# HGRN recurrence of a hybrid decoder step: eight slots a head joined to five

## The reference

```
b = jnp.cumsum(gc, axis=1)
o_inter = jnp.einsum('bthk,bhkv->bthv', qc * jnp.exp(b), S)
decay = jnp.where(tri, jnp.exp(jnp.where(tri, diff, 0.0)), 0.0)      # diff = b_t - b_s
att = jnp.einsum('bthk,bshk,btshk->bhts', qc, kc, decay)
o_intra = jnp.einsum('bhts,bshv->bthv', att, vc)
S = jnp.exp(b_last)[..., None] * S + jnp.einsum('bshk,bshv->bhkv', kc * jnp.exp(b_last[:, None] - b), vc)
```

## Time and profile before

| | us |
|---|---|
| median of 3 runs | 1181.65 |
| lowest and highest | 1181.28, 1184.76 |
| span of the profiled execution | 1185.2 |
| PE busy | 1123.6 (95%) |
| DVE busy | 703.2 (59%) |
| ACT busy | 536.1 (45%) |
| POOL busy | 172.4 (15%) |

### The profile page before, as it was taken

One profiled execution on the slowest core, in us unless ns is written; L12 is line 12 of the kernel. 1 busy time (PEld: TensorE's weight loads), 2 busy tenths in 40 slices (PEclk: granted clock), 3 DMA queues, 4 the chain that ended last, 5 costly groups with the idle time before them and its releaser, 6 DMA issues.

```text
span 1185.2 us, 21987 instructions
## 1 busy us (share of the span) xinstructions
PE 1123.6 (95%) x8805; PEld 1059.3 (89%) x8805; DVE 703.2 (59%) x1440; ACT 536.1 (45%) x951; POOL 172.4 (15%) x137
## 2 busy tenths in 40 slices
PE   5898999998999989999999999899999999999997
PEld 4797889876899978989989999699999999999997
DVE  5735555445487767477788554736464555537465
ACT  3433556465546664755555423543323232232324
POOL 1400000000132213213121001321101010010101
PEclk9899999988999989999999999899999999999998
DMA  9884333212322311221322373032322322322202
GB/s 309 268 291 139 109 106 107 74 37 71 116 90 75 109 54 61 69 84 63 110 64 73 100 251 113 2 108 72 105 74 72 107 72 72 97 81 72 73 35 81
DMA packets 108922, 120.53 MB, mean 102 GB/s; under 512 B 2708, under 2 KB 98796, under 8 KB 108533
## 3 DMA queue, kind: packets, MB, share of 16 engines
q1 hardware_dynamic: 108821, 119.13, 31.1%
HBM read 109.29 MB, written 11.80 MB: 102 GB/s over the span
## 4 chain that ended last, share of the span: by engine, by line
PE 45%; DVE 3%; ACT 1%; issue 1%; POOL 0%; DVEq 0%; ACTq 0%; POOLq 0%
PE PS L860 41%; PE PS L833 1%; DVE wR L1448 1%; PE PS L983 0%; PE PS L773 0%; PE PS L782 0%; DVE tmp L1432 0%; PE PS L1055 0%; PE PS L806 0%; POOL hR L1767 0%; ACT wR L1116 0%; DVE xhat L1416 0%; DVE xT L1465 0%; PE PS L1022 0%; ACT hR L1185 0%
## 5 line engine op out<-in xcount | busy, mean ns | idle before, releaser
L860 PE MATMUL PS<-hR,wR 128*128 128x288 f32 x3744 | 528.4, 299 | 1.9 <-DVE mods L1476 1.0
L860 PEld LDWEIGHTS PS<-hR,wR 128*128 128x128 f32 x3744 | 505.6, 189 | 11.6 <-issue 9.6
L1448 DVE TENSOR_TENSOR wR<-raw,wR 128x512 fp32r<-128x512 f32 x260 | 213.6, 821 | 84.5 <-ACT wR L1116 77.2
L860 PE MATMUL PS<-actR,wR 128*128 128x288 f32 (+2 forms) x1920 | 260.9, 297 | 1.8 <-DVE actR L1596 1.8
L860 PEld LDWEIGHTS PS<-actR,wR 128*128 128x128 f32 x1920 | 257.0, 189 | 3.0 <-DVE actR L1596 2.0
L1116 ACT ACTIVATE wR<-raw 128x512 fp32r<-128x512 f32 x260 | 164.3, 632 | 141.6 <-PE PS L860 132.9
L1782 POOL TENSOR_TENSOR D<-b 128x512 f32<-128x512 f32 (+1 forms) x48 | 59.5, 1239 | 484.6 <-PE PS L948 264.2
L1809 POOL TENSOR_TENSOR actR<-tmp,actR 128x576 fp32r<-128x576 f32 x32 | 46.3, 1448 | 304.7 <-DVE actR L1511 304.7
L1511 DVE CAST actR<-tmp 128x576 fp32r<-128x576 f32 x32 | 15.2, 476 | 125.7 <-ACT tmp L1227 125.7
L815 PE MATMUL PS<-wR,hR 128*128 128x256 f32 x600 | 78.9, 288 | 0.0
L815 PEld LDWEIGHTS PS<-wR,hR 128*128 128x128 f32 x600 | 74.4, 193 | 2.1 <-issue 1.7
(11 more groups left out here) (227 smaller groups left out, 1189.4 us busy)
## 6 DMA issues: line engine op xcount, KB each, us to landing
raw<-in_w_in SPq DMA_DIRECT2D x30, 1024.0 KB, 5.1
raw<-in_w_up SPq DMA_DIRECT2D x16, 1024.0 KB, 5.5
raw<-in_w_down SPq DMA_DIRECT2D x16, 1024.0 KB, 4.9
mid<-in_w_ada SPq DMA_DIRECT2D x12, 1024.0 KB, 5.0
ada<-in_w_ada SPq DMA_DIRECT2D x8, 1024.0 KB, 11.9
S<-in_state_hgrn SPq DMA_DIRECT2D x8, 512.0 KB, 4.4
out_hgrn_sample<-S SPq DMA_DIRECT2D x8, 512.0 KB, 4.9
raw<-in_w_out SPq DMA_DIRECT2D x4, 1024.0 KB, 5.1
```

Source lines behind the costliest of these rows:

```text
L860: mm = pe.matmul(PS[:, 2 * x.pair + h, 0:size], weights(x, w, k, col), rhs[r], start=(k == 0 and n == 0), stop=(k == last and n == 2))
L1448: done(dve.tensor_tensor(w[:, 1, cols], raw[SLOT[SPLITS[n]]][:, cols], w[:, 0, cols].bitcast(F32), ALU.subtract), s_lo)
```

## The change

Only `hgrn_slots` changes. Before, each head has eight slots: one for each level, with the other events hung on them, one of the two sample halves with level 5 and the other with the output, then the norm. Now a head has five: the diagonal with levels 0 and 1 and `g_hats`; levels 2 and 3 with the keys; level 4, the state and level 5; both sample halves with the output; the norm. One of the two empty slots at the start of a pair is gone too, so that a pair has 13 slots in place of 20, spread over the same chunks. Within a level the order of the events is kept, and so is the distance, counted in levels, at which operands, exponents and differences run ahead.

```
-        for k in range(NL + 2):
-            ev = []
-            if k == 0:
-                ev += [("g_diag", r)]
-            if k < NL:
-                n = (r - first) * NL + k
...
-            if k == 1:
-                ev += [("g_hats", r)]
-            if k == 3:
-                ev += [("g_keys", r)]
-            if k == 4:
-                ev += [("g_state", r)]
-            if k in (5, 6):
-                ev += [("g_sample", r, k - 5)]
...
+        def level(k):
+
+            n = (r - first) * NL + k
+            ev = [("g_operands", *at(n + 1))] if n + 1 < 2 * NL else []
+            if k == 2:
+                ev += [("g_products", r)]
+            ev += [("g_level", r, k)]
+            if n + 2 < 2 * NL:
+                ev += [("g_exp", *at(n + 2))]
+            if n + 3 < 2 * NL:
+                ev += [("g_diff", *at(n + 3))]
+            return ev
...
+        yield [("g_diag", r)] + level(0) + ([("g_scale", first)] if r == second else []) + level(1) + [("g_hats", r)]
+        yield level(2) + level(3) + [("g_keys", r)]
+        yield level(4) + [("g_state", r)] + level(5)
+        yield [("g_sample", r, 0), ("g_sample", r, 1), ("g_out", r)] + ([("g_start", second)] if r == first else [])
+        yield [("g_norm", r)] + ([("g_scale", r)] if r == second else [])
```

More of the change, by code:

```diff
@@ L216, in hgrn_slots @@
     yield []
-    yield []
     for r in (first, second):
+        def level(k):
[9 more added lines that the diff above has]
+            return ev
         if r == second:
             yield []
-        for k in range(NL + 2):
-            ev = []
-            if k == 0:
-                ev += [("g_diag", r)]
-            if k < NL:
-                n = (r - first) * NL + k
[L227 to L237, removed]
-            if k == 1:
-                ev += [("g_hats", r)]
-            if k == 3:
-                ev += [("g_keys", r)]
-            if k == 4:
-                ev += [("g_state", r)]
-            if k in (5, 6):
-                ev += [("g_sample", r, k - 5)]
[L246 to L254, removed]
+        yield [("g_diag", r)] + level(0) + ([("g_scale", first)] if r == second else []) + level(1) + [("g_hats", r)]
[3 more added lines that the diff above has]
+        yield [("g_norm", r)] + ([("g_scale", r)] if r == second else [])
 def walk():
```

## The result

The changed kernel takes 1218.41 us, the median of four runs (1215.18 to 1220.40); the kernel before, on the same chip, 1181.55. The ratio is 1.0305, with a 95% interval of 1.0283 to 1.0326. The sign of the prediction was right, its size was not: +36.9 us where +14.6 were worked out, and outside the range. In the later series the kernel before took 1183 to 1186 us, so some 3 us of the 36.9 are uncertain.

A forecast was written before the change was run, and what follows sets the result against it. PE bounds the HGRN stretch, losing 20.1 us to waits and clock. Idle +12.9 and clock +1.7 make +14.6 us; added to the 1181.65 us median, 1196 us, range 1182 to 1207.

The forecast's parts named there:

- Where the time goes: In the stretch where HGRN slots run, time moves only with PE's idle time and clock: together +14.6 us.
- The mechanism: At joined slots, the second level directly follows the first on PE, with no chunk covering DVE's operands: idle +12.9 us.
- The rival that the change covers its own chains: Second slots' distance covers both table-load chains and all of level 5: 1176 us, chance 0.12.
- the one in which DVE runs ahead at level 5: At level 5 only head 2's 3.4 us of 9.3 remain: 1190 us, chance 0.12.
- The sum of the waits: PE's idle time at levels 1, 3 and 5: 11.3 + 3.9 + 9.3 = 24.5 us, against 11.6 before.
- DVE has nothing late ahead of the slot: At level 1 of heads 1, 2, 4, 5, 6 and 7, each waits 1.2 us: 7.2 us.
- where no tile ends between ... DVE has the operands before PE comes: At level 3, no wait there or where three chunks lie between; only head 4 waits, 3.9 us.
- The clock: PE's lost clock time in the stretch, 10.2 us against 8.5 before: +1.7 us.
- the four counted falls: Clock loss behind PE waits of 2.3 and 1.8 us, 1.7 each, and 3.4 and 3.9 us, 3.4 each: 10.2 us.
- clock 1.00 around the 1.2 us waits: At level 1, waits near 1.2 us leave PE at full clock, costing no clock time.
- rival (a): Small PE waits lower the clock too, nine waits of 1.2 to 1.45 us costing 1.7 each: 1211 us, chance 0.08.
- The samples and the table loads: Moved samples cost nothing; table loads take 1.28 us without the page's extra drain, which would add 8.3 us.

The follow-up runs named there:

- kernels 9 and 10: Changed kernel with second levels one chunk later, ratio 1.0064; kernel before with levels 0, 2, 4 directly ahead of 1, 3, 5 in old places, ratio 1.0312.
- Experiment 6: Kernel before with only levels 2 and 3 joined, all else unchanged: 1202.95 us, ratio 1.0154.
- kernel 2: Changed kernel with level 1's operands moved ahead of the diagonal on DVE: 1207.98 us, ratio 1.0194.
- kernel 4: Changed kernel (five slots) with operands, exponents and differences running one level further ahead: 1206.59 us, ratio 1.0183.
- kernel 11: Kernel before with operands, exponents and differences one level further ahead, and keys, state and samples one slot later: 1191.37 us, ratio 1.0061.
- kernel 12: Kernel before with operands, exponents and differences one level further ahead, plus g_hats and g_products one level earlier in each pair's first head: 1173.80 us, ratio 0.9914.
- kernel 1: Kernel before with only both sample halves moved into the output's slot: 1184.60 us, ratio 0.9996.

## Why the prediction was right in sign and wrong in size

**Where the time goes.** Right. The stage is 32.8 us longer; the remaining difference of the spans is the start, 3.6 us earlier, and the end, 1.0 shorter. The stage's idle time and lost clock time rose by 20.4 + 13.6 = 34.0. The 1.2 us too many are low clock during waits, which stands in both terms. The medians differ by 36.9, the spans by 28.2 only, because neither profiled execution is a typical one. A run's time is 1.8 us above its span wherever both are given, so the profiled execution of before would be one of about 1187 us (an estimate), 5.4 above its median; that of after is the fastest of its four, 3.2 below. The 4 us between the stage and the medians lie within that spread; in which part of the program they arise stays open.

**The mechanism.** Right, and shown: the second level waits for DVE because no chunk stands between (kernels 9 and 10). The rival that the change covers its own chains falls, and so does the one in which DVE runs ahead at level 5: 10.1 us stand there.

**The sum of the waits.** Predicted 24.5 us of idle time, measured 32.0. Where I had followed DVE's list to the slot, the numbers held: of thirteen such places twelve lie within 0.25 us, the chains with table loads among them (3.39 for 3.4, 4.13 for 3.9). The step that failed is "DVE has nothing late ahead of the slot", said of heads 6 and 7 without a row for it, and "where no tile ends between ... DVE has the operands before PE comes" at level 3. Heads 6 and 7 gave 3.03 and 2.29 in place of 1.2, and level 3 of heads 1, 3 and 5 gave 3.7 in place of nothing. Together 6.6 of the 7.5 us. In heads 6 and 7 `lo` and evacuations hold the diagonal on DVE. At level 3 it is, by the timeline, ACT's wait at `g_hats`, which the prediction had followed in head 4 alone, and the longer instructions beside POOL, which it had not reckoned with. Experiment 6 is the sharper form of it: the join that I took for nearly free costs 11.2 us of idle time when it stands alone.

**The clock.** This is the term that failed most: +1.7 predicted, +13.6 measured. The two prices were good: seven of the falls after cost about 1.7 us, three about 3.4, as with the 1.7 and 3.4 that I took from the earlier trace rows. That the four counted falls cost 10.2 us as predicted is in part luck: head 2's wait of 3.39 us cost 1.7 in place of 3.4, and head 3's of 1.98 cost 3.4 in place of 1.7. The number of falls was wrong: four were counted, ten came. Of the other six, 12.0 us together, four (8.6 us) came behind waits that the sum had too short or not at all: 3.03 and 2.29 at level 1 of heads 6 and 7, 1.67 and 1.39 at level 3 of heads 1 and 3. Two (3.4 us) came behind waits that it had about right and without a fall, 1.42 and 1.02 (at 556). So the larger part of the clock's error follows from the missed waits, the smaller from "clock 1.00 around the 1.2 us waits".

Among the waits without a fall are two others of 1.02, and 1.45, 1.49 and 1.85 us (at 526; both windows from 525 to 535 show clock 1.00). The stretch of 7 us with two waits and clock 1.00 in the earlier trace rows, which I had set against rival (a), is one of the cases without a fall, and I read it as the rule. So rival (a) is partly right, and it is not the length of a single wait that decides; what does was not found. The Trainium skill, "TensorE: Matmul & The Clock Gate", section "A second HAM failure mode: psum-queue depth-cycling", describes another kernel in which frequent short idle times between groups of matmuls make the clock go back and forth. The trace agrees, with ten falls in place of four; which idle times bring a fall the section does not say, and here eight of the 18 waits left the clock alone.

**The samples and the table loads.** Both held. The sigmoid of head 2's tile starts 1.29 us behind its table load, as in the earlier trace rows. The Trainium skill, "ScalarE: Activation LUTs", section "What ACT_TABLE_LOAD costs", would add about 1.38 us of drain to each of that chain's two switches; as an estimate from that page the wait would have been 3.4 + 2.8 = 6.2 us. It was 3.39.

## What to carry to other kernels

Before two dependent steps of one engine are put side by side, ask what the work between them was covering: here a chunk of 1.6 us on PE hid a round trip over DVE, and its loss at 24 places cost 2.4%. A wait taken away at one place of an engine that works through a list in order shows up again at the next item of the list, unless the chain that feeds it is shortened too; kernel 2 lost about half of its gain that way, kernel 4 most of it and kernel 11 all of it, and kernel 12 kept it by starting the whole chain earlier. When many waits of about a microsecond are to arise, price the clock of each as lost until rows show otherwise (ten of 18 lost it here).

## What the runs showed of the hardware that was not expected

The clock fell to its lower level (1.2 of 2.4 GHz) behind single waits of 1.0 to 1.7 us in a stream that was otherwise busy, and each fall cost about 1.7 or about 3.4 us. A wait of 1.85 us passed without one. The same length can go either way even at the same place: the wait of 3.16 us in head 2 of the earlier trace rows cost 3.4 us of clock, and in kernel 1 the same wait left the clock up, so that the eight matmuls behind it take 1.13 us in place of 2.04:

```profile
424.27 1.13 PE L979 MATMUL PS<-D,kt 128*128 128x128 f32 x8 [3.15 <-DVE att L1639]
```

DVE's instructions grew beside POOL's. In head 1 the evacuation, begun at 375.04, took 1.40 us and the operand, begun at 376.48, took 1.25, against 0.76 and 0.42 where POOL was quiet. POOL's instruction of 374.39 ran until 375.83, its difference from 375.91 to 377.45; an operand that started only then would have ended at 377.87, and it ended at 377.73. The Trainium skill, "SBUF — State Buffer", section "Who interferes with whom", says that these two engines share one pair of ports, that a DVE instruction with both inputs in SBUF meets POOL's reads there, and that the second to come is blocked until the first has done; the end of the operand agrees to 0.14 us. No run took POOL's work away to test it.
